# Expert items with one size tree on PE only, its nodes running matmuls, and straight code at 336 columns on VectorE and ScalarE

## The reference

```python
logits = xt @ w_router
top_v, top_i = top_k(logits, 2); top_w = softmax(top_v)
order = argsort(top_i.reshape(-1)); xs = xt[order // 2]
h = silu(ragged_dot(xs, wg, sizes)) * ragged_dot(xs, wu, sizes)
ys = ragged_dot(h, wd, sizes) * top_w.reshape(-1)[order][:, None]
y = zeros_like(xt).at[order // 2].add(ys)
```

## Time and profile before

| | us |
|---|---|
| median of 3 runs (lowest, highest) | 5370.12 (5369.08, 5370.41) |
| span of the profiled execution | 5373.2 |
| PE busy in it | 4993.1 |
| DVE busy | 3328.4 |
| ACT busy | 1582.4 |

### The profile page before, as it was taken

The page is one execution under the profiler, slowest core; times in us unless marked ns, Lnnn a source line. Parts: engine busy times, 40 slices in busy tenths (PEclk is TensorE's granted clock), DMA queues, the critical chain, the costliest instruction groups (busy, mean ns, idle before and its releaser), DMA issues.

```text
span 5373.2 us, 87186 instructions
## 1 busy us (share of the span) xinstructions
PE 4993.1 (93%) x33128; PEld 4918.7 (92%) x33129; DVE 3328.4 (62%) x5292; ACT 1582.4 (29%) x2280; POOL 421.9 (8%) x254
## 2 busy tenths in 40 slices
PE   8999999999998999999879798998989898979969
PEld 7999999999998999999769797998989797979958
DVE  5677655554447666875657565665667575756665
ACT  2112222111113211122234333333334343433333
POOL 3111101101102211110010000000000000000020
PEclk8999999999999999999979898999999899989979
DMA  3111111111111111111155454444445454544431
GB/s 99 43 43 40 40 45 40 48 40 48 47 41 45 45 49 43 39 41 47 39 192 179 145 164 141 143 145 139 152 155 183 156 184 158 185 133 158 147 120 40
DMA packets 399071, 529.06 MB, mean 98 GB/s; under 512 B 12056, under 2 KB 353606, under 8 KB 398616
## 3 DMA queue, kind: packets, MB, share of 16 engines
q1 hardware_dynamic: 359552, 460.75, 26.4%
q0 software_dynamic: 11136, 33.97, 1.9%
q10 hardware_dynamic: 27928, 28.60, 1.6%
HBM read 494.87 MB, written 28.39 MB: 97 GB/s over the span
## 4 chain that ended last, share of the span: by engine, by line
PE 40%; issue 5%; DVE 3%; DMA 2%; ACT 1%; ACTq 0%; DVEq 0%; POOL 0%; POOLq 0%; SPq 0%
PE PS L682 9%; PE PS L684 9%; PE PS L683 9%; PE PS L786 4%; PE PS L787 4%; PE PS L788 4%; DMA WRAW<-in_moe_w_gate 1%; DVE XSL L2144 1%; DVE EACC L2202 0%; PE PS L981 0%; DVE WLO L1469 0%; ACT WHI L1089 0%; PE PS L1041 0%; PE PS L970 0%; DMA XG<-sorted_rows 0%
## 5 line engine op out<-in xcount | busy, mean ns | idle before, releaser
L1469 DVE TENSOR_TENSOR WLO<-WRAW,WHI 128x1024 fp32r<-128x1024 f32 x866 | 1066.7, 1233 | 352.7 <-ACT WHI L1089 228.7
L682 PE MATMUL PS<-XSH,WHI 128*128 128x256 f32 (+5 forms) x3584 | 1070.9, 299 | 151.3 <-issue 151.3
L682 PE MATMUL PS<-XHI,WHI 128*128 128x384 f32 (+1 forms) x3648 | 1202.8, 330 | 3.9 <-DVE ACC L1978 2.4
L684 PE MATMUL PS<-XHI,WLO 128*128 128x384 f32 (+1 forms) x3648 | 1197.3, 328 | 0.0
L683 PE MATMUL PS<-XLO,WHI 128*128 128x384 f32 (+1 forms) x3648 | 1196.8, 328 | 0.0
L1089 ACT ACTIVATE WHI<-WRAW 128x1024 fp32r<-128x1024 f32 x866 | 898.7, 1051 | 959.2 <-PE PS L788 670.4
L683 PE MATMUL PS<-XSL,WHI 128*128 128x256 f32 (+5 forms) x3584 | 1067.8, 298 | 0.0
L684 PE MATMUL PS<-XSH,WLO 128*128 128x256 f32 (+5 forms) x3584 | 1065.4, 297 | 2.0 <-issue 2.0
L682 PEld LDWEIGHTS PS<-XSH,WHI 128*128 128x128 f32 x3584 | 685.1, 191 | 155.3 <-issue 155.3
L682 PEld LDWEIGHTS PS<-XHI,WHI 128*128 128x128 f32 x3648 | 691.2, 189 | 7.5 <-DVE ACC L1978 3.2
L683 PEld LDWEIGHTS PS<-XLO,WHI 128*128 128x128 f32 x3648 | 691.1, 189 | 0.7
(11 more groups left out here) (368 smaller groups left out, 5934.1 us busy)
## 6 DMA issues: line engine op xcount, KB each, us to landing
WRAW<-in_moe_w_gate SPq DMA_DIRECT2D x112, 1024.0 KB, 5.0
WRAW<-in_moe_w_up SPq DMA_DIRECT2D x112, 1024.0 KB, 5.0
WRAW<-in_moe_w_down SPq DMA_DIRECT2D x112, 1024.0 KB, 4.9
WRAW<-in_w_in SPq DMA_DIRECT2D x48, 1024.0 KB, 5.2
WRAW<-in_ffn_w_gate SPq DMA_DIRECT2D x11, 1024.0 KB, 5.4
WRAW<-in_ffn_w_up SPq DMA_DIRECT2D x11, 1024.0 KB, 5.3
WRAW<-in_ffn_w_down SPq DMA_DIRECT2D x11, 1024.0 KB, 5.0
XG<-sorted_rows POOLq DMA_DIRECT2D x18, 512.0 KB, 7.2
```

Source lines behind the costliest of these rows:

```text
L682: pe.matmul(PS[:, bank, 0:n], wh, hi(k), start=(k == 0), stop=False)
L684: ins = pe.matmul(PS[:, bank, 0:n], wl, hi(k), start=False, stop=(k == KC - 1))
L1469: v.do(dve.tensor_tensor(WLO[s][:], raw_view(conv.n // 2 % RAW, conv.n % 2, kind), WHI[s][:].bitcast(F32), ALU.subtract), conv)
```

## The change

`sized` is gone. DVE and ACT run each item as straight code, all 14 groups written out, always at 336 columns; DVE's first DN step copies into EACC where it added, so that POOL's clear of EACC, and the two waits that came with it, are gone. POOL waits for `xg_used` alone before it issues the loads of XG.

PE keeps a tree of the same shape, but its nodes run parts of the item. Going in, the node at depth 0, 1, 2 and 3 runs unit 0, 1, 2 and 3 of GU0 ahead of its `If`s, with the widest size below it, and the first three also the transposes of `item_out`. A leaf holds the loop of six iterations and two units of GU13. Going out, behind either half, the node at depth 3 runs the other two units of GU13, at depth 2 the first four tiles of DN12 with four `prepare`s, at depth 1 its other four, at depth 0 the first four tiles of DN13, with the widest size of the half that was run. A leaf at depth 3 runs the part of depth 3 itself. Behind the tree the last four tiles of DN13 run at 336 columns.

```diff
             with g.If(it < n_items):
-                g.wait_ge(S["ys_full"], it * 3 + 3)
-                spacer(g)
-                g.memset(EACC[:], 0.0).then_inc(S["sums_clear"], 1)
-
                 row = g.value_load(ITEMS[0:1, bass.ds(it + L_ROW + 2, 1)], min_val=0, max_val=PAIRS)
                 g.wait_ge(S["xg_used"], it + 1)
...
-                        def item(rows):
...
+                        def begin(rows, depth):
+
+                            gate_up(rows, depth)
+                            if depth < len(XBLK):
+                                item_out(depth)
+
+                        def end(rows, depth):
+
+                            if depth == 3:
+                                gate_up(rows, 2)
+                                gate_up(rows, 3)
+                            elif depth == 2:
+                                pe.wait_ge(S["xg_ready"], it * 48 + 96)
+                                add_down(rows, last - 1, range(0, 4), prepare)
+                            elif depth == 1:
+                                add_down(rows, last - 1, range(4, KC), prepare)
+                            else:
+                                add_down(rows, last, range(0, 4))
...
+                            gate_up(rows, 0)
+                            gate_up(rows, 1)
+                            for x in range(3, depth - 1, -1):
+                                end(rows, x)
+
+                        def choose(low, high, depth):
+
+                            if depth < 4:
+                                begin(SIZES[high - 1], depth)
+                            if high - low == 1:
+                                item(SIZES[low], depth)
+                                return
+                            middle = (low + high) // 2
+                            here = [c.n for c in cs]
+                            with pe.If(size < middle):
+                                choose(low, middle, depth + 1)
+                                end(SIZES[middle - 1], depth)
+                            for c, n0 in zip(cs, here):
+                                c.n = n0
+                            with pe.If(size > middle - 1):
+                                choose(middle, high, depth + 1)
+                                end(SIZES[high - 1], depth)
+
+                        pe.wait_ge(S["split_done"], hs.take(KC))
+                        choose(0, len(SIZES), 0)
+                        add_down(CAP, last, range(4, KC))
...
+                                    if g == 0:
+                                        v.do(dve.tensor_copy(a, ps[:, 0:CAP]), q)
+                                    else:
+                                        v.do(dve.tensor_tensor(a, ps[:, 0:CAP], a, ALU.add), q)
...
+                        first, *middle, late, last = list(groups(MOE_GROUPS))
+                        step(*first, between=lambda u: item_out(it, u) if u < len(XBLK) else None)
+                        for s in middle:
+                            step(*s)
+                        step(*late, between=prepare)
+                        step(*last)
```

More of the change, by code:

```diff
@@ L135, in leave_items @@
         c.terms.append((reg, per[c]))
[L138 to L154, removed]
 def build(nc, A, O):
@@ L990, in _ @@
                         st = looped(cs, it, per)
-                        def item(rows):
[L993 to L1008, removed]
+                        q_item = q.at(q.n)
@@ new lines, in _, with gate_up, add_down @@
+                        last = MOE_GROUPS - 1
+                        def gate_up(rows, u):
+                            use()
+                            b = open_bank()
+                            product(b, rows, unit.n % HL, lambda k: XSH[:, k, 0:rows], lambda k: XSL[:, k, 0:rows]).then_inc(q.next(), 1)
+                            unit.n += 1
+                        def add_down(rows, g, outs=range(KC), after=lambda d: None):
+                            if 0 in outs:
+                                pe.wait_ge(S["split_done"], hs.take(2))
+                            down(EHI[g % 2], ELO[g % 2], ((0, rows),), after, outs)
@@ L1009, in item @@
+                        def item(rows, depth):
+                            for u in range(depth + 1, 4):
+                                begin(rows, u)
                             head, body, tail = ffn_schedule(MOE_GROUPS, MOE_LOOP)
-                            for s in head:
-                                step(*s, after=lambda u: item_out(u) if u < len(XBLK) else None)
                             with pe.Fori(0, MOE_LOOP) as i:
@@ L1334, in conv @@
                             convert()
[L1336 to L1350, removed]
+                        kp[0] = LOOK
@@ L1351, in step @@
+                        def step(kind, g, between=lambda: None):
+                            if kind == "GU":
+                                for f in range(2):
                                     conv()
[L1352 to L1353 removed]
+                                    q.n += 1
+                                    serve(lambda: act.activation(EG[:, f, :], EG[:, f, :], ACT.Silu))
+                                for f in range(2):
@@ L1367, in item @@
-                            leave(cs2, st2, per2, MOE_LOOP)
-                            kp[0] += 12 * (MOE_LOOP - 1)
-                            step(*tail[0])
-                            step(*tail[1], between=lambda: [prepare(k) for k in range(KC)])
-                            step(*tail[2])
-                        sized(act, size, cs, item)
+                                    q.n += 1
+                                    act.wait_ge(S["split_req"], split.at(split.n + 1))
+                                    act.activation(EHI[g % 2][:, f, :], T[split.n % 2][:, 0:CAP], ACT.Copy).then_inc(split.next(), 1)
+                            else:
+                                conv()
+                                between()
+                                q.n += KC
+                                conv()
@@ L1374, in _ @@
+                        first, *middle, late, last = list(groups(MOE_GROUPS))
+                        step(*first)
+                        item_out(it, row)
+                        m.n += 6
+                        for s in middle:
+                            step(*s)
+                        step(*late, between=lambda: [prepare(k) for k in range(KC)])
+                        step(*last)
                         leave_items(cs, st, per, n_items)
```

116 lines of the change are left out of this document (42 added, 74 removed).

## The result

The changed kernel takes 5336.99 us (median of 4 runs, 5332.57 to 5342.29) against 5369.6 for the kernel before on the same chip: ratio 0.9941, 95% interval 0.9928 to 0.9954. That is 33 us faster, where 85 were forecast (5285 us): the right sign, under half the size. The profiled execution has a span of 5340.7 us (before 5373.2).

What follows compares the result with a forecast made beforehand. PE was taken as bound, with time to gain only at item boundaries, filled by jumps (163 us). 65 - 12 + 16 + 16 = 85 us gained gave 5285 us; own range 5255 to 5315 (chance 0.50), 8 in 10: 5205 to 5352.

Steps and rivals of the forecast that it cites:

- the clock: PE at item boundaries: slow matmuls also cover the next jump, so half an estimate was kept, 16 us gained.
- the jumps: PE's nodes and back-edges: work at the nodes covers jumps, 98 us of gaps where 163 stood, 65 us gained.
- Widths: PE's nodes use the widest size below them: 1168 extra columns over groups of 24 matmuls, 12 us lost.
- DVE and ACT straight and wide: DVE and ACT lose their trees and work at 336 columns everywhere; PE covers the added width: 0 us.
- The stall for the weight tile: POOL fetches XG earlier, in the tail of the item before; of 21.2 us of PE stalls 5 stay: 16 us gained.
- part 3: DVE and ACT without trees at 336 columns: straight code streams and PE covers the width, 0 us.
- part 1: PE's nodes do work at item boundaries, covering part of each jump: 98 us of gaps for 163, 65 us gained.
- rival of hardly any cover: PE's nodes: waits inside them leave the queue all but empty at each branch, 154 us of gaps, 5347 us; chance 0.14.
- bounds of the cover: PE's jumps: 44 us of gaps stay with the FFN back-edge's lead everywhere, 154 with next to no cover.
- slower: Rival: hardly any cover, and the clock drops over both ends of every item; about 5480 us, 5400 if half; chance 0.09.
- step 5: PE's clock at the boundaries: half kept, 16 us gained, between 30 and a loss.
- No 6 us ones: Sign in the changed trace: PE's far branches still 36 and 3.5 to 4 us long, none of 6 us.

Runs made afterwards that it cites:

- e7: Changed kernel with DVE's copies and adds into EACC cut from 336 to 256 columns: 5334.44 us, ratio 0.9938.
- e1: PE's section as in the kernel before, with its whole tree; DVE, ACT and POOL as in the changed kernel: 5354.98 us, ratio 0.9969.
- e9: Changed kernel with POOL fetching XG in three parts in the middle of the item, not in its tail: 5326.36 us, ratio 0.9924.
- e4: Changed kernel with PE's node cuts moved, so each branch follows 24 matmuls and the transposes come behind it: 5314.73 us, ratio 0.9891.
- e10: Changed kernel with more of the item's work in PE's nodes and XG fetched in the middle of the item: 5299.12 us, ratio 0.9872.
- e8: Changed kernel with no tree: PE takes every item as straight code at 336 columns: 5542.16 us, ratio 1.0323.
- e3: Changed kernel with fourteen semaphore increments on PE's sequencer ahead of each of a node's two branches: 5402.04 us, ratio 1.0051.
- e2: PE as in the changed kernel; DVE and ACT keep their trees at 336 columns, POOL its clear of EACC: 5440.2 us, ratio 1.0131.

## Why the prediction was right and wrong

In the order of its steps, the profiled executions set side by side. The forecast was a gain of 85; the phase gained 34 (2409 to 2375). Two terms carry the miss: the clock, +16 where -14 to -21 came, and the jumps, +65 where +51 came.

- **Widths, -12.** Right: the matmuls at pace went from 2135.1 to 2147.4, by 12.3 us.
- **DVE and ACT straight and wide, 0.** Right as far as it was tried: e7 for the adds, and ACT's "issue" waits of 22.4 us in eight pieces of at most 5.8, hidden under PE's first unit.
- **The stall for the weight tile, +16.** Right and a little low: all 21 us are gone, and e1 gives 17 us by itself. But the step looked only at whom XG's new place helps. It also said the fetch falls "in the tail, where PE's jumps give it room", and that was the mistake: each long jump has a packet of queue 8 of its own, and with XG beside them five of them took 1.5 to 3.1 us longer than in e9. e9 puts the price at 11 us net.
- **The jumps, +65.** 163 us of jump gaps became 112, not 98. Some 94 of these lie at jumps, and there the sum held, though by terms that cancel: a unit of 24 matmuls is handed over in 1.0 to 1.4 us and not 2.2, which brings the next branch on earlier, and the branches are 3.3 to 6.4 us long, not 3.7. The step that failed is that the sum has no stall of straight code behind a landing (part 3 says of DVE and ACT that "Straight code streams", part 1 takes it for PE; before 2700 us the kernel before shows no "issue" wait on DVE, but 18 on ACT with 24.2 us in sum): 18 us are the five gaps of that kind, which no row that I had read showed. The trace of the kernel before does hold a small one, 2.05 us at 3664.62, two matmuls behind the landing at 3661.69. Beside them the short lead ahead of the entry jumps, which the prediction had seen ("The transposes' wait for DVE's copies keeps the lead short there"), was probably priced too low: e4, which takes it away, gave 22 us, but with them come shorter branches and, in the profiled executions, the 6 us at the exit.
- **The clock, +16.** Wrong in sign, and the largest miss: matmuls took 37.4 us above their pace before and 51.2 after, and the rest, mostly transposes, went from 42.2 to 48.9. No run shows the 16: it was kept as half of an estimate for the slow clock of the kernel before, of which the table has 37.4 us. Where +16 stood it is -14 for the matmuls, or -21 with the rest. The argument was that slow matmuls in a chain of nodes also cover the next jump. Some do; but there are 35 gaps over 1 us where there were 19, and the matmuls behind them are now wide ones at work. The windows at 4216.95 and 4228.77 above show it: PE busy for all of 3.00 us at a granted clock of 0.50 (1.00 is full speed), 14 and 13 matmuls where the pace of the earlier trace rows at 336 columns makes 20. e1 shows that it is PE's nodes that bring this: without them, 28.1. The kernels with less gap time than the changed one have less of it (e4 44.6, e9 46.9, e10 36.9, e8 18.3), e3 with more has 67.2. Neither the time nor the number of gaps gives it alone: before has 182 us of gaps and 37.4 of it, e2 203 and 56.1, and e9 has 39 gaps over 1 us where the changed kernel has 35.

Sum: -12 for widths, +21 for the stall, +51 for the jumps, -21 for clock and transposes, -3 for the start of the first item, which lies outside the phase as counted, and some -2 not placed: 34. The rival of hardly any cover came nearest in time (5347), but not in mechanism: the cover was there and the clock ate a part of the gain.

Three sums of the prediction do not come out as they stand. The jumps were counted as 36, with "7 jumps" in the gap of 29.77 us, but one of these seven took 0.23 us, as the earlier trace rows shows (229 ns), and the trace has 33 long ones, 4.9 us each. The bounds of the cover are 39 and 149 us by their own prices (28 x 0.8 and 8 x 2.1; 28 x 4.0 and 8 x 4.6), not 44 and 154; with the 8 us of the last exit and the 1 us of the first item's start they come to 46 and 153. And 5480 for "slower" holds only if the 30 us of slow clock (the upper end of step 5) that the kernel has already are taken off. None of them moves the forecast by more than some 7 us.

Of what the prediction said would show: no "issue" gap of 20 us, many of 1 to 4 (a few up to 5.3, and 13.1 at the exit), DVE up by 82 us, XG earlier: so in the main. ACT's gaps reach 5.8 us where 5 was the limit, and PE's waits that name EACC sum to more than 8 us, though they are jumps. "No 6 us ones" among the branches was wrong, and for a reason that the earlier trace rows already held. The 6.12 us of 4508.86 was read as "one right on another's heels"; its successors stood just as close and took 4.9. The DMA share of the stretch would have told it: in the kernel before, the second branch of a boundary and a later one, each within 0.2 us of its forerunner:

```profile
2994.67:2997.67 3.00, 0.00 (x0) 0.00 (x0) 0.98 (x1) 0.00 (x0) 0.00 (x0) 0.57 1.00 330
3318.47:3321.47 3.00, 0.00 (x0) 0.00 (x0) 0.00 (x0) 0.00 (x0) 0.00 (x0) 0.50 0.13 19
```

They take 6.71 and 4.94 us.

Closeness does add something when it is very close: branches that start within 0.4 us of the end of the one before take 4.7 to 5.3 us even at a share of 0.17 or less (the kernel before has 14 of them). The queues show what differs there, two packets of queue 8 instead of one. During the branch at 4515.03 of the kernel before, 4.93 us long:

```profile
q8 instruction: 2, 0.03, 4.8%
q14 instruction: 5, 0.04, 4.8%
```

The 5.79 us at 5095.87 in the changed kernel, at a share of 0.07 and 0.75 us behind another branch, has three. At 1.3 us behind another no such addition is seen in e9 (3.76 to 3.94 us at a share of 0.03), but two back-edges of e3, 2.2 us behind another, have two packets as well and take 5.3 and 5.1 us at a share of 0.45 and 0.37. So closeness is not all that brings a second packet.

Open: no run isolates what brings these second packets. Nor did I try to move the weights or the output rows away from the branches that stay long, or to take away the gap behind a landing (in e9 those five are 1.5 to 2.2 us, so load is a part of it).

## What to carry to other kernels

A far jump costs PE what the work handed over ahead of it does not cover, and that was 2.8 us here, 18 or 19 matmuls, of a jump of 3.65: put at least so many that wait for nothing ahead of it, and keep transfers that are not urgent out of the stretch where engines jump, or behind code that has just landed. Count the gaps over 1 us, not only their sum: the matmuls behind them ran slower, at a granted clock of 0.50 in the earlier trace rows and in the windows at 4216.95 and 4228.77. By the table a gap brings 1.5 to 2 us of it (37.4 us behind 19 gaps, 51.2 behind 35), so by estimate one gap of 20 us costs 22 and six of 3 us cost 27; no run sets the two against each other. Where a wait names an engine that had been done for a microsecond, lay the branches beside it before believing it, and for a branch or a gap on "issue" the packets of queue 8.

## What the hardware showed unexpectedly

The length of a far branch of PE goes with the DMA load beside it: it takes mostly 3.3 to 4.0 us with the DMA engines less than half busy, mostly 5 to 6.7 at a share of 0.9 and more, and 3.76 against 5.84 us for one and the same branch when the fetch of XG beside it was moved (e9). In 33 of the 35 long branches of the changed kernel's expert phase one packet of queue 8 (16.4 KB, by 4.05 MB in 247) moves, and it starts 0.9 to 1.6 us behind the branch at a share under 0.5 and 3.0 to 3.8 us behind it at 0.9 and more; the branch ends 2.3 to 2.9 us later in either case. That the branch waits for this packet of instructions, and the packet for the kernel's own transfers, is how I read these times.

Straight code behind a landing can stall too: 2.9 to 4.3 us after six matmuls, with no branch running, in five boundaries of the changed kernel, each time with a packet of queue 8 that starts 2.3 to 2.6 us ahead of the matmul that ends the gap. With one copy of the item instead of eleven (e8) neither shows: no branch of the expert items over 0.26 us, no wait of PE on "issue", 6 such packets instead of 109. And a bare semaphore increment costs PE's sequencer 0.15 us (e3), so fourteen of them eat 2.1 of the 2.8 us of lead that hide most of a jump.
